# Dilated attention by tiles of two heads with its projections in pieces, and products of ones by ones in TensorE's waits

## The reference

```python
qkv = (x @ w_qkv).reshape(B, S, 3, 3, 16, 64)          # 3 dilations x (q, k, v) x 16 heads x 64
# for each dilation: windowed attention with distance slopes, scores masked outside the window
outs, lses = per dilation
w = softmax(lses over the 3 dilations)
out = (sum of w * outs).reshape(B, S, 1024) @ w_out
```

## Time and profile before

| | |
|---|---|
| median of 3 runs | 3557.4 us (3556.03 to 3557.8) |
| the profiled execution | 3555.88 us |
| its span in the profile | 3554.1 us |
| TensorE busy | 3406.6 us, 96% |
| VectorE, ScalarE, GpSimd busy | 1494.2, 824.8, 2509.9 us |
| mean granted clock of TensorE | 0.990 |

### The profile page before, as it was taken

The page is one execution under the profiler, slowest core; times in us unless marked ns, Lnnn a source line. Parts: engine busy times, 40 slices in busy tenths (PEclk is TensorE's granted clock), DMA queues, the critical chain, the costliest instruction groups (busy, mean ns, idle before and its releaser), DMA issues.

```text
span 3554.1 us, 48351 instructions
## 1 busy us (share of the span) xinstructions
PE 3406.6 (96%) x18548; PEld 2824.0 (79%) x18548; DVE 1494.2 (42%) x2315; ACT 824.8 (23%) x1463; POOL 2509.9 (71%) x2220
## 2 busy tenths in 40 slices
PE   7999989999999999989898999989999998999998
PEld 6887878888888888878787888877778787777876
DVE  6653463112311152341626213365756525565643
ACT  1110233110211022231324211121332312232321
POOL 7998787888788876447374788856556785656675
PEclk9999999999999999999999999999999999999999
DMA  5553222222232222112121232222222222222222
GB/s 183 186 186 114 79 86 92 94 92 94 87 94 93 98 89 90 48 60 83 37 95 37 86 102 95 88 86 72 66 60 69 78 89 81 66 67 71 59 89 72
DMA packets 322426, 312.06 MB, mean 88 GB/s; under 512 B 11568, under 2 KB 306128, under 8 KB 322000
## 3 DMA queue, kind: packets, MB, share of 16 engines
q1 hardware_dynamic: 304928, 277.91, 25.0%
q10 hardware_dynamic: 17328, 31.78, 2.7%
HBM read 307.56 MB, written 2.10 MB: 87 GB/s over the span
## 4 chain that ended last, share of the span: by engine, by line
PE 45%; issue 28%; POOL 20%; DVE 4%; ACT 1%; POOLq 0%; DMA 0%; SPq 0%; DVEq 0%; ACTq 0%
PE ps L1759 16%; POOL wh L346 14%; PE ps L384 12%; POOL wl L350 7%; PE ps L1515 4%; PE ps L557 3%; PE ps L1802 2%; PE ps L2335 1%; PE ps L859 1%; PE ps L531 1%; PE ps L2136 1%; DVE at_sc L1427 1%; PE ps L2107 1%; PE ps L2121 1%; DVE at_nb L1443 0%
## 5 line engine op out<-in xcount | busy, mean ns | idle before, releaser
L346 POOL TENSOR_TENSOR wh<-w_raw,zero 128x512 fp32r<-128x512 f32 (+3 forms) x1108 | 1146.7, 1045 | 1013.4 <-PE ps L384 460.4
L350 POOL TENSOR_TENSOR wl<-w_raw,wh 128x512 fp32r<-128x512 f32 (+3 forms) x1108 | 1420.9, 1293 | 0.0
L384 PE MATMUL ps<-xh,wh 128*128 128x512 f32 x1888 | 738.6, 391 | 6.8 <-DVE at_ol L1560 4.5
L384 PE MATMUL ps<-xh,wl 128*128 128x512 f32 x1888 | 734.9, 389 | 0.0
L384 PE MATMUL ps<-xl,wh 128*128 128x512 f32 x1888 | 734.8, 389 | 0.0
L384 PEld LDWEIGHTS ps<-xh,wh 128*128 128x128 f32 x1888 | 354.5, 188 | 83.2 <-ACT at_qk L1528 5.2
L384 PEld LDWEIGHTS ps<-xh,wl 128*128 128x128 f32 x1888 | 354.4, 188 | 74.0
L384 PEld LDWEIGHTS ps<-xl,wh 128*128 128x128 f32 x1888 | 354.6, 188 | 73.4 <-issue 1.0
L1117 DVE TENSOR_TENSOR ps<-sg,ps 128x512 f32<-128x512 f32 x88 | 61.2, 696 | 590.9 <-PE ps L384 563.2
L1759 PE MATMUL ps<-xh,wh 128*128 128x512 f32 x688 | 288.9, 420 | 5.4 <-POOL wl L350 2.6
L1759 PE MATMUL ps<-xh,wl 128*128 128x512 f32 x688 | 271.3, 394 | 0.0
(11 more groups left out here) (357 smaller groups left out, 6155.8 us busy)
## 6 DMA issues: line engine op xcount, KB each, us to landing
w_raw<-in_w_in SPq DMA_DIRECT2D x120, 512.0 KB, 4.1
w_raw<-in_ffn_w_gate SPq DMA_DIRECT2D x88, 512.0 KB, 4.7
w_raw<-in_ffn_w_up SPq DMA_DIRECT2D x88, 512.0 KB, 4.7
w_raw<-in_attn_w_qkv SPq DMA_DIRECT2D x72, 512.0 KB, 4.2
w_raw<-in_ffn_w_down SPq DMA_DIRECT2D x64, 512.0 KB, 3.6
ada_raw<-in_ada_w ACTq DMA_DIRECT2D x24, 512.0 KB, 3.9
stats<-in_ada_w ACTq DMA_DIRECT2D x24, 512.0 KB, 3.9
w_raw<-in_ffn_w_down SPq DMA_DIRECT2D x32, 384.0 KB, 4.0
```

Source lines behind the costliest of these rows:

```text
L346: done.append(s["w_hi"].up(pool.tensor_tensor(hi[:, parts[q]], raw[:, parts[q]], zero, ALU.subtract)))
L350: s["w_lo"].up(pool.tensor_tensor(lo[:, parts[q]], raw[:, parts[q]], hi[:, parts[q]].bitcast(F32), ALU.subtract))
L384: mm = self.nc.tensor.matmul(out, a[:, slot, w], b(t), start=start and t == order[0] and q == 0, stop=stop and t == order[-1] and q == 2)
```

## The change

**Attention.** The unit is now a tile of two heads. Its projections are five chunks for an even tile and four for an odd one: three chunks with q in one half and k in the other for the three dilations, one with the values of the first two dilations, and for even tiles one with the values of the third dilation for both tiles. The columns of w_qkv are put into that order on the host, before the launch. `pe_attn_project` is a generator that gives the work of a tile in pieces, eight per half: one k step of three products, or six products of the values. Within pair i, TensorE takes pieces of the next tile's projections between the pair's steps. For the last tile they are the first 14 pieces of the output projection. ScalarE's evictions and VectorE's low parts are put at fitting places of their queues. q, k and low parts have two buffers by tile, the transposes have two PSUM banks (one far, one near) instead of three, and the values product has one bank.

**Ones.** `pe_spin` multiplies the tile of ones by itself n times into a PSUM bank that is free. It stands in `pe_first`, five times before each of the first two tiles (not in the first stage), and in `pe_entry`, fourteen times after each half's sums of squares.

```diff
+    def pe_spin(self, bank, at, n):
+        out = self.ps[:, bank, at:at + P]
+        for _ in range(n):
+            self.nc.tensor.matmul(out, self.ones[:], self.ones[:], start=True, stop=True)
...
     def pe_first(self, pe, st, residue=False):
...
                     if n == 0:
+                        if h == 0 and k < 2 and before.kind != "start":
+                            self.pe_spin(self.VAR_BANK[1], 0, 5)
                         pe.wait_ge(s["acts"].sem, st.at("acts", KT * h + k + 1 - 2 * KT))
...
     def pe_entry(self, pe, st):
...
             s["e_var"].up(mm)
+            if h:
+                self.pe_spin(2, 0, 14)
             if h == 0:
                 pe.wait_ge(s["lin_ev"].sem, st.at("lin_ev", 0))
+                self.pe_spin(0, 0, 14)
...
-    def pe_out(self, pe, st, c1, xs, before=None, residue=False):
+    def pe_out(self, pe, st, c1, xs, before=None, residue=False, begun=0):
...
-                self.product(pe, (c1 + pair) % 2, KT, 256, m * P, self.ps[:, n % 4], xs, before=before if n == 0 else None)
+                done = begun if pair == 0 else 0
+                self.product(pe, (c1 + pair) % 2, KT, 256, m * P, self.ps[:, n % 4], xs, start=not done, before=before if n == 0 else None, order=range(done, KT))
...
     def pe_attn_turn(self, pe, st, i, hh):
...
-        for step in ((near, far) if hh else (far, near)):
-            step()
+        if hh == 0:
+            if i:
+                pe.wait_ge(s["pt_copied"].sem, st.at("pt_copied", 3 * i))
+            far()
+            near()
+        else:
+            near()
+            pe.wait_ge(s["pt_copied"].sem, st.at("pt_copied", 3 * i + 1))
+            far()
...
+    def pe_attn_begin_out(self, pe, st):
+        s, c = self.s, st.chunk0 + 9 * QUADS
+        arrive = self.arrival(pe, c, KT)
+        for m, ks in ((0, range(6)), (1, range(6)), (0, (6,)), (1, (6,))):
+            pe.wait_ge(s["lin_ev"].sem, st.at("lin_ev", 18 * QUADS - 1 + m))
+            for t in ks:
+                if m == 0:
+                    arrive(t)
+                pe.wait_ge(s["o_lo"].sem, st.at("o_lo", t + 1))
+                self.piece(c % 2, 256, m * P, self.ps[:, m], self.heads_out(), (t,), t == 0, False)
+                yield
...
+    def attn_halves(i):
+        tile, n = divmod(i, 4)
+        if tile + 1 >= KT:
+            return 0
+        return 2 if tile % 2 == 0 or n > 1 else 3
...
+    def pe_attn(self, pe, st):
+        s = self.s
+        self.pe_first(pe, st, True)
+        fill = self.pe_attn_project(pe, st, 0, 2)
+        for _ in range(3 * 8):
+            next(fill)
+        self.pe_attn_scores(pe, st, 0)
+        for _ in fill:
+            pass
+        for i in range(ATTN_PAIRS + 1):
+            tile = i // 4
+            pieces = 8 * self.attn_halves(i)
+            if pieces and i % 4 == 0:
+                fill = self.pe_attn_project(pe, st, tile + 1)
+            if i == ATTN_PAIRS - 4:
+                fill = self.pe_attn_begin_out(pe, st)
+            if i >= ATTN_PAIRS - 4:
+                pieces = 3
+            parts = (2, 6, pieces - 8) if pieces > 8 else (1, 1, 1)
+            if i:
+                self.pe_attn_turn(pe, st, i - 1, 0)
+            for _ in range(parts[0]):
+                next(fill, None)
+            if i:
+                self.pe_attn_turn(pe, st, i - 1, 1)
+            if i + 1 < ATTN_PAIRS:
+                self.pe_attn_scores(pe, st, i + 1)
+            for _ in range(parts[1]):
+                next(fill, None)
+            if i:
+                self.pe_attn_out(pe, st, i - 1)
+            for _ in range(parts[2]):
+                next(fill, None)
...
     def act_attn(self, act, st):
...
+        for i in range(ATTN_PAIRS + 1):
+            tile, at = divmod(i, 4)
+            if i:
+                for n in range(3):
+                    self.act_attn_turned(act, st, i - 1, n)
+            if i < ATTN_PAIRS:
+                for hh in range(2):
+                    self.act_attn_probs(act, st, i, hh)
+            first = sum(self.attn_halves(4 * tile + k) for k in range(at))
+            for n in range(first, first + self.attn_halves(i)):
+                self.act_attn_half(act, st, tile + 1, n // 2, n % 2)
+                if n == 0 and i:
+                    self.act_attn_o_hi(act, st, tile - 1)
+            if at == 0 and i >= ATTN_PAIRS - 4:
+                self.act_attn_o_hi(act, st, tile - 1)
...
     def dve_attn(self, dve, st):
...
+            if i:
+                self.dve_attn_norm(dve, st, i - 1, 1)
+            if at == 1 and self.attn_halves(i - 1) == 2:
+                self.dve_attn_qk_low(dve, st, tile + 1, (1,))
+            if i < ATTN_PAIRS:
+                self.dve_attn_near(dve, st, i)
+                self.dve_attn_far(dve, st, i, 1)
```

More of the change, by code:

```diff
@@ L1473, in pe_attn_half @@
-        if j % 3 < 2:
-            self.product(pe, c % 2, KT, 256, m * P, self.ps[:, m], self.x_parts(), before=arrive)
-        else:
-            self.values(pe, c % 2, 256, 0, 256, m, *self.x_tiles(), before=arrive)
+        pe.wait_ge(s["lin_ev"].sem, st.at("lin_ev", n - 3 if (tile, j) == (0, 2) else n - 1))
+        if j == (1 if tile else 2):
+            pe.wait_ge(s["qk_low"].sem, st.at("qk_low", 2 * tile + m + 1))
+        if j < 3:
+            for t in range(KT):
+                if arrive:
+                    arrive(t)
+                mm = self.piece(c % 2, 256, m * P, self.ps[:, m], self.x_parts(), (t,), t == 0, t == KT - 1)
+                if t == KT - 1:
+                    s["acc"].up(mm)
+                yield
+            return
```

237 lines of the change are left out of this document (120 added, 117 removed).

## The result

Over four runs of each kernel the median is 3501.81 us (3499.56 to 3501.97) against 3556.89 (3556.03 to 3557.8): the ratio is 0.9844, interval 0.9831 to 0.9856. The gain is 55.1 us, forecast were 61. The profiled execution took 3499.56 us with a span of 3497.7, so all that follows reads 56.4 us of span.

What follows compares the result with a forecast made beforehand. TensorE was taken as the bound, with attention pairs paced by VectorE. Gains of 55 us (61 − 2 − 3.5) and 6.7 us sum to 61.7, from the median 3557.4 to 3496 us; range 3486 to 3524.

Steps and rivals of the forecast that it cites:

- Part 1: Attention stage: projection pieces between the pairs' steps cover TensorE's waits on VectorE and ScalarE; gain 55 us.
- 4.33 + 16 × 0.68 = 15.2 us, or 20.6 with 24 pieces: Attention: TensorE's time for one pair's turn, its own steps plus pieces of three 512-column products at 0.68 us each.
- the 61 counted: Attention before the change: TensorE's idle time including hidden waits, 15.3 us per quad, 61 us in four.
- 2 + 3.5: Attention idle time expected to remain: 2 us in four stalls at even tiles, 3.5 us at tile 7.
- 1.6 us against a copy of 0.60: Attention: two pieces and two near transposes cover head 1's far transposes' wait for head 0's copy from the shared bank.
- Part 2: Stage borders and mixer entries: products of ones fill waits and keep TensorE's clock full; gain 6.7 us.
- The two borders: FFN 0 to pool and FFN 2 to attention: removing 3.6 us half-clock windows gives 3.5 us.
- The entries: Two mixer entries: full clock gives 1.2 us in the second half and 0.9 in the first, 4.2 in all.
- rival 2: Pieces work, but ones do nothing or get in the way, idle remainders being left: 3502 to 3507 us; 12%.
- (1): Attention: pieces leave one hand-over per pair in TensorE's way, 29 us lost, 3525 us; 15%.
- (3): Attention: GpSimd's weight split becomes the bound through VectorE blocking it, slower at 3600 us; 3%.
- (4): Attention: pieces stand behind the same waits as before, nothing won, 3557 us; 2%.

Runs made afterwards that it cites:

- blocks of a tile: Changed kernel with all projections of the next tile in one stretch in each tile's third pair, none between other pairs' steps: 3578.9 us.
- one block: Changed kernel with all pieces of a pair behind the values product, none between the two heads' transposes: 3512.05 us.
- two blocks and more ones: Changed kernel with no pieces between scores and values, and 6 ones at borders, 21 and 17 at entry halves: 3494.56 us.

## Why the prediction was right, point by point

**The time** came out 5.8 us above the forecast, 3501.8 against 3496, inside its range.

**Part 1, 55 us forecast; 47.6 in the profile**, being 49.1 in the attention stage less the 1.6 us that its border gained by the clock (its first 96 products take 16.59 us instead of 18.20 from start to start); by medians 48.9. The mechanism is as predicted: the waits once per pair are gone, VectorE and ScalarE are done in time, and laying the steps apart is what does it (blocks of a tile).

The term that was mis-sized is the pieces in a pair's turn, "4.33 + 16 × 0.68 = 15.2 us, or 20.6 with 24 pieces". The turn takes 15.6 to 16.1 and 21.1. The 4.33 was nearly right (4.24); the 0.68 per piece holds inside a long row of q or k products only. Changes between products and scores or values add some tenths to a turn, which the sum had at nothing, and over the stage the products take 11.8 us more than before. The turns exceed the forecast by more than that, 137.6 us for a period of eight against 132.4, some 18 us in 28 turns; but 6 of these are the values' own price of 0.72 per piece in 10 turns, which the kernel before pays as well.

The idle time was counted well. At 4.24 us a pair, 32 pairs need 135.7 us; their steps took 197.5 before, so 61.8 were idle, against the 61 counted. This holds although the turn of 5.54 us that the count was read from is the shortest of a quad: its seven turns, from scores to scores, are 7.41, 5.62, 6.33, three of 5.54, and 6.81 us. After, 2.4 of these are left, where 2 + 3.5 were forecast: the four stalls at even tiles did not come, and tile 7 waits for 0.6 and 0.5 us in one pair, whose turn is 8.05 us, and for 1.5 us behind the last values product. So 59.3 were won where 55.5 were forecast, 11.8 were lost where nothing was, and the forecast came as near as it did partly because the two errors point opposite ways.

Two smaller readings of the prediction are wrong. The 36 weight chunks of the attention projections come in 72 DMAs of 512 KB, not 36, in both kernels. And VectorE's work left out the biases, 32 operations of 1.02 us on average in the stage; the pieces cover them.

**The covers.** "1.6 us against a copy of 0.60", the far transposes of head 1, held; with the pieces taken out, the wait appears 27 times (one block).

**GpSimd and VectorE.** GpSimd kept up: 1053 ns an operation against 1045. VectorE's scaling did grow beside it, by (1003 − 692) × 2 = 0.62 us per pair on average, under the bound of 1.3 from the rows, though single ones of 1.72 are longer than the 1.26 that the bound took as the longest. In the Trainium skill (SBUF — State Buffer, "Who interferes with whom") the one of such a couple that comes second waits for the other's whole instruction; the trace agrees: the 22 scalings with no GpSimd operation beside them took 0.62 us, and the 42 with one 0.62 to 1.72. As forecast it stayed hidden below the pair's 15.2 us.

**Part 2, 6.7 us forecast, 6.4 and 7.0 measured** by medians. That the sum fits so well is partly luck, since the places fit less. The two borders had 3.5 forecast; measured without ones against after they gave 0.9 at pool and 1.2 in attention, and in the kernel before 0.8 and 1.5. Without ones 1.6 more are lost at FFN 2, a border that had no such window in the kernel before. The entries had 4.2 forecast, and gave 4.3 after and 5.8 before. The subtracted 1 us for borders with short waits did not appear: with the ones and without, FFN 1 and FFN 3 agree within 0.2 us in the kernel after, though the ones do leave no wait there. The price of a product of ones, "0.22 us", was right: 3.04 / 14 = 0.22 and 1.03 / 5 = 0.21. The remainder after the ones, the doubt of rival 2, did not matter at the borders; at mixer 0's first half it left a window at 0.53, which cost nothing.

**The rivals.** A wait once per pair (1) is refuted by the list of waits; ones without effect (2) by both runs on them, though 3501.8 lies just at the edge of its times, for another reason; the split as the bound (3) by GpSimd's rows; a change without effect (4) by the stage's length.

## What to carry to other kernels

Where one engine waits often and briefly for others, lay independent work between the steps themselves: the same work in tile-sized stretches brought the waits back, and cost 78 us more. Then count the changes between kinds of product, and put the filling where a change costs nothing (here beside transposes, not between scores and values), keeping only the pieces that cover a wait. Filling waits to keep TensorE's clock up brought 6.4 and 7.0 us here while the filling was shorter than nearly every wait; measure the wait first, since what went beyond it was paid in full. And add up a trace from start to start before giving a difference to a cause: in one block, 16.8 us of waits showed as 8.1 of idle time.

## What the runs showed of the hardware that I had not expected

- A change of products costs TensorE time without a row of idle: 0.32 to 0.34 us for the first 512-column product of a block, 0.32 for the last one ahead of scores or values, 0.227 in the steady state, and 0.23 and 0.03 ahead of and behind a transpose.
- Stretches of 3.6 or 7 us at a granted clock of 0.53 come and go elsewhere with the moment at which a stage begins: the border of pool and FFN 1 lost 1.6 us in three of the experiments (378.0 instead of 376.4 us in the table) with the same five ones in place, FFN 3 lost 1.2 to 1.5 us in the kernel before, with one block and with two blocks and more ones, and one window near 474 us stood in the kernel before and in all versions. What sets that is open.
- VectorE's scaling took 1003 ns on average instead of 692, and the difference goes with GpSimd's work: 0.62 us in each of the 22 with no GpSimd operation beside them, 1.20 on average in the 42 with one. A short operation suffers more: the biases, 128 x 128, took 0.29 us alone and 1.12 on average beside GpSimd.
